# Down projections of a two-block transformer kernel: both classic output tiles in front of the Winograd groups in each first part

## The reference

```python
def sq_relu_mlp(x, w1, w2):
    h = jax.nn.relu(x @ w1)      # w1: 1024 x 4096
    return (h * h) @ w2          # w2: 4096 x 1024
```

```python
def swiglu(h, w_gate, w_up, w_down):          # width 2816
    return (jax.nn.silu(h @ w_gate) * (h @ w_up)) @ w_down
```

## Time and profile before

| | |
|---|---|
| median of 3 runs | 2046.54 us (2044.86 to 2048.42) |
| the profiled execution, its own time | 2046.04 us |
| its span in the trace | 2044.2 us |
| mean granted TensorE clock | 0.988 of full speed |
| PE, DVE, ACT busy | 96%, 70%, 46% of the span |
| DMA queues | 27.9% of 16 engines for the weights, mean 88 GB/s |

### The profile page before, as it was taken

How to read it: one execution, slowest core, us unless ns; L and a number is a source line. 1 busy time by engine, 2 the same in 40 slices (tenths; PEclk the granted TensorE clock), 3 DMA queues, 4 the chain that set the end, 5 groups by cost and what they waited for, 6 DMA issues and landing times. The chain is left out here.

```text
span 2044.2 us, 29741 instructions
## 1 busy us (share of the span) xinstructions
PE 1958.9 (96%) x11816; PEld 1070.4 (52%) x11821; DVE 1421.9 (70%) x2445; ACT 947.8 (46%) x1628; POOL 71.4 (3%) x51
## 2 busy tenths in 40 slices
PE   9989999999999999999999999999989999999997
PEld 4444444444444874444445844854544444476466
DVE  6979644548677677676587767769866646965777
ACT  4447733324333343346454434436467844643442
POOL 2000000000000102000000000000000000100000
PEclk9999999999999999999999999999989999999999
DMA  7300233324331343222221532316300031324321
GB/s 245 99 1 1 73 102 98 99 71 125 110 95 32 117 144 110 77 83 73 73 88 63 176 93 61 126 53 175 147 1 1 14 101 42 98 93 155 93 63 42
DMA packets 53931, 179.55 MB, mean 88 GB/s; under 512 B 6176, under 2 KB 11936, under 8 KB 53536
## 3 DMA queue, kind: packets, MB, share of 16 engines
q1 hardware_dynamic: 53792, 177.64, 27.9%
HBM read 174.47 MB, written 2.10 MB: 86 GB/s over the span
## 5 line engine op out<-in xcount | busy, mean ns | idle before, releaser
L2182 DVE SCALAR_TENSOR_TENSOR w_lo<-w_raw,w_hi 128x1024 f16<-128x1024 f32 (+3 forms) x359 | 452.1, 1266 | 82.9 <-ACT w_hi L1736 47.7
L1736 ACT ACTIVATE w_hi<-w_raw 128x1024 f16<-128x1024 f32 (+1 forms) x358 | 373.5, 1063 | 223.1 <-DVE w_raw L2202 84.6
L1171 PE MATMUL pS<-xx,w_hi 128*128 128x512 f16 x952 | 362.0, 380 | 5.1 <-DVE w_lo L2182 3.7
L1172 PE MATMUL pS<-xx,w_hi 128*128 128x512 f16 x952 | 362.0, 380 | 0.0
L1173 PE MATMUL pS<-xx,w_lo 128*128 128x512 f16 x952 | 361.9, 380 | 0.0
L1239 PE MATMUL pS<-arena,w_hi 128*128 128x256 f16 x645 | 178.0, 276 | 11.7 <-DVE arena L2775 5.1
L1241 PE MATMUL pS<-arena,w_lo 128*128 128x256 f16 x645 | 178.1, 276 | 0.0
L1240 PE MATMUL pS<-arena,w_hi 128*128 128x256 f16 x645 | 178.1, 276 | 0.0
L1171 PEld LDWEIGHTS pS<-xx,w_hi 128*128 128x128 f16 x952 | 93.4, 98 | 114.6 <-issue 5.6
L1173 PEld LDWEIGHTS pS<-xx,w_lo 128*128 128x128 f16 x952 | 93.3, 98 | 113.2 <-issue 1.5
L1172 PEld LDWEIGHTS pS<-xx,w_hi 128*128 128x128 f16 x952 | 93.3, 98 | 108.1 <-issue 1.9
(11 more groups left out here) (455 smaller groups left out, 3821.2 us busy)
## 6 DMA issues: line engine op xcount, KB each, us to landing
w_raw<-in_w SPq DMA_DIRECT2D x299, 512.0 KB, 3.8
w_raw<-in_w SPq DMA_DIRECT2D x12, 704.0 KB, 4.0
X<-in_x SPq DMA_DIRECT2D x8, 264.0 KB, 6.4
arena<-in_c SPq DMA_DIRECT2D x2, 1024.0 KB, 7.5
out_t<-X SPq DMA_DIRECT2D x16, 128.0 KB, 1.7
arena<-in_h SPq DMA_DIRECT2D x4, 256.0 KB, 12.5
arena<-in_h SPq DMA_DIRECT2D x2, 512.0 KB, 11.4
arena<-in_c SPq DMA_DIRECT2D x2, 256.0 KB, 2.9
```

The costliest lines, as they stand in the source:

```text
L1171: pe.matmul(ps, wh, ah, start=f, stop=False)
L1172: pe.matmul(ps, wh, al, start=False, stop=False)
L1736: act.activation(to_, from_, ACT.Copy, scale=WS).then_inc(hi_split, 1)
L2182: dve.scalar_tensor_tensor(out=lo_[:, a:], in0=from_[:, a:], scalar=WS, in1=hi_[:, a:], op0=ALU.mult, op1=ALU.subtract).then_inc(lo_split, 1)
```

## The change

- **a parts** (dn0a, dn1a): tile 7 becomes the second tile of the first classic stage. PE's order is now: tile 0, k 0 to 13; the second classic tile ("tile 1" of that stage), k 0 to 6; tile 0, k 14 and 15; the second tile, k 7 to 15; the three groups. Nothing stands behind the groups.
- **b parts and ffd**: tile 0 up to the last pair of k; product A11 of group 0, all but its last tile of k; tile 0's last pair; the rest of A11; the groups; tile 7 in halves as before.
- **Banks**: tile 0 of all five goes to bank 5 (pO), the second classic tile of the a parts to bank 3 (BANKS).
- **Weights**: the last unit of ffd7, up0a and up1a is closed at the stage's end (CLOSED), so the next stage starts a unit of its own. In the weight stream tile 7 of an a part stands behind tile 0.
- **Norms**: AHEAD["mb"] is 4 instead of 8, and in all of them the copy of the second half stands in front of the look-ahead splits instead of behind them (`formed`, the copy, `split_lo` instead of `out_of`, the copy).
- **Bias row**: `lay_bias` stands behind group 0 of dn0b on DVE, its high half there on ACT; ACT's wait for all operands ahead of a b part is gone.

The diff, cut where it only takes out what the functions above show:

```diff
@@ -74,3 +74,4 @@
 INSIDE = {"va": 0, "vb": NQ, "vm": 0, "vv": 0}
-BEHIND = ("dn0a7", "dn1a7")
+BANKS = {"ffd0": (5,), "dn0a0": (5, 3), "dn1a0": (5, 3), "dn0b0": (5,), "dn1b0": (5,)}
+CLOSED = ("ffd7", "up0a", "up1a")
 UP_A = 16
@@ -159,3 +160,4 @@
                     for kk in range(k):
-                        self.step(self.tau, kk == k - 1)
+                        ends = name in CLOSED and j == n - 1 and kk == k - 1
+                        self.step(self.tau, kk == k - 1, ends)
             else:
@@ -206,4 +208,4 @@
                     b = 4 + j if j < 2 else turn % 4
-                elif s.name in BEHIND:
-                    b = 4
+                elif s.name in BANKS:
+                    b = BANKS[s.name][j]
                 elif s.name in HOME:
@@ -275,4 +277,5 @@
 
-    def step(self, tau, last):
+    def step(self, tau, last, close=False):
         self.tile()
+        self.open = self.open and not close
         ends = not self.open
@@ -301,3 +304,5 @@
     k = UP_A if part == "a" else KFF2 - UP_A
-    return [(f"dn{lay}{part}0", "T", 1, k, 1), (f"dn{lay}{part}s", "S", 3, k // 2, 1), (f"dn{lay}{part}7", "T", 1, k, 1)]
+    if part == "a":
+        return [(f"dn{lay}a0", "T", 2, k, 1), (f"dn{lay}as", "S", 3, k // 2, 1)]
+    return [(f"dn{lay}b0", "T", 1, k, 1), (f"dn{lay}bs", "S", 3, k // 2, 1), (f"dn{lay}b7", "T", 1, k, 1)]
 
@@ -330,3 +335,3 @@
 DIRECT = ("x2", "ma", "mb", "mc", "md")
-AHEAD = {"x2": 8, "ma": 2, "mb": 8, "mc": 2, "md": 8}
+AHEAD = {"x2": 8, "ma": 2, "mb": 4, "mc": 2, "md": 8}
 HALVED = tuple(AHEAD)
@@ -1222,21 +1227,20 @@
 
-            def strassen(s, g, ops, copies, r):
...
+            def product(s, g, x, ops, copies, k0, k1):
+
+                name, b, op = PRODUCTS[x]
+                free = s.banks[g][b]
+                if name == "A12":
+                    pe.wait_ge(first_copied, copies + g + 1)
+                elif k0 == 0 and free >= 0:
+                    pe.wait_ge(evicted, free + 1)
+                ps = (pS[:, b, 0:HT] if b < 4 else (pT, pO)[b - 4][:, 0, 0:HT])
+                a = slice(op * HT, op * HT + HT)
+                for k in range(k0, k1):
+                    tau = s.factor(g, x, k)
+                    wh, wl = weights(tau)
+                    oh, ol = ops[0][:, k, a], ops[1][:, k, a]
+                    pe.matmul(ps, wh, oh, start=k == 0 and name != "A12", stop=False, skip_group_check=True)
+                    pe.matmul(ps, wh, ol, start=False, stop=False, skip_group_check=True)
+                    mm = pe.matmul(ps, wl, oh, start=False, stop=k == s.k - 1, skip_group_check=True)
+                if k1 == s.k:
                     mm.then_inc(mm_done, 1)
@@ -1249,9 +1253,19 @@
 
-                for k in range(parts[0].k):
-                    out_pair(parts[0], by_pairs(ops), k, r)
+                s, n = parts[0], parts[0].k
+                for k in range(n - 2):
+                    out_pair(s, by_pairs(ops), k, r)
+                if m is None:
+                    tile_T(s, 1, by_pairs(ops), 0, TPU - 1)
+                else:
+                    product(parts[1], 0, 0, ops, copies, 0, n // 2 - 1)
+                for k in range(n - 2, n):
+                    out_pair(s, by_pairs(ops), k, r)
+                if m is None:
+                    tile_T(s, 1, by_pairs(ops), TPU - 1, n)
                 for g in range(parts[1].n):
-                    strassen(parts[1], g, ops, copies, r + parts[0].k)
-                if m is None:
-                    out_T(parts[2], 0, by_pairs(ops))
-                else:
+                    for x in range(len(PRODUCTS)):
+                        if g == 0 and x == 1:
+                            pe.wait_ge(rhs_ready, r + n)
+                        product(parts[1], g, x, ops, copies, n // 2 - 1 if m is not None and g == 0 and x == 0 else 0, n // 2)
+                if m is not None:
                     out_last(parts[2], m, by_pairs(ops))
@@ -1260,14 +1274,5 @@
 
...
+                tile_T(s, 0, rhs, k, k + 1)
 
@@ -1652,3 +1657,3 @@
                     out_T(S[f"up{lay}a"], j, xr)
-                down([S[f"dn{lay}a{n}"] for n in "0s7"], hp, PL.r[h], 3 + 6 * lay)
+                down([S[f"dn{lay}a{n}"] for n in "0s"], hp, PL.r[h], 3 + 6 * lay)
                 for j in range(KFF2 - UP_A):
@@ -1748,3 +1753,4 @@
 
-                out_of(parts[0])
+                for j in range(parts[0].n):
+                    out_of(parts[0], j)
                 if m is not None:
@@ -1761,5 +1767,6 @@
                             square(PL.q[m] + n, out_to(m, n))
-                if m is None:
-                    out_of(parts[2])
-                else:
+                    if g == 0 and m == "mb":
+                        act.wait_ge(bias_laid, 1)
+                        hi(PL.r["pe"], z[0][:, 2, :], src[:, 1, :])
+                if m is not None:
                     halved_norm(parts[2], m)
@@ -2097,8 +2104,4 @@
                 up_part(S[f"up{lay}a"], lay, r, 0)
-                down([S[f"dn{lay}a{n}"] for n in "0s7"], 3 + 6 * lay, 1.0 / WS)
+                down([S[f"dn{lay}a{n}"] for n in "0s"], 3 + 6 * lay, 1.0 / WS)
                 up_part(S[f"up{lay}b"], lay, r, UP_A)
-                if lay == 0:
-                    act.wait_ge(bias_laid, 1)
-                    hi(PL.r["pe"], z[0][:, 2, :], src[:, 1, :])
-                act.wait_ge(rhs_ready, r + KFF2 + (lay == 0))
                 down([S[f"dn{lay}b{n}"] for n in "0s7"], 6 + 6 * lay, 1.0 / WS, m)
@@ -2807,4 +2810,5 @@
                 s = parts[0]
-                out_of(s)
-                taken_to(m, out_to(m, 0), out_bank(s.o0), f, to_add).then_inc(evicted, 1)
+                for j in range(s.n):
+                    out_of(s, j)
+                    taken_to(m, out_to(m, (0, KD - 1)[j]), out_bank(s.o0 + j), f, to_add).then_inc(evicted, 1)
                 s = parts[1]
@@ -2815,7 +2819,7 @@
                             add_square(m, n)
+                    if g == 0 and m == "mb" and squares:
+                        lay_bias()
+                if not squares:
+                    return
                 s = parts[2]
-                if not squares:
-                    out_of(s)
-                    taken_to(m, out_to(m, KD - 1), out_bank(s.o0), f, to_add).then_inc(evicted, 1)
-                    return
                 for n in (KD - 3, KD - 2):
@@ -2832,5 +2836,7 @@
                 if n == AMONG["x2"]:
-                    ps = out_of(s)
+                    formed(s, 0)
+                    ps = out_bank(s.o0)
                     dve.scalar_tensor_tensor(out=X[:, KD - 1, HT:T], in0=ps[:, HT:T], scalar=0.5 / WS, in1=X[:, KD - 1, HT:T],
                                              op0=ALU.mult, op1=ALU.add).then_inc(evicted, 1)
+                    split_lo(PL.out_tau[s.o0], most=splits(s, 0))
                 if n == KD - 1:
@@ -2937,3 +2943,3 @@
 
-                        out_of(s, s.n - 1)
+                        formed(s, s.n - 1)
                         if s.n == KD:
@@ -2941,2 +2947,3 @@
                         taken_to(m, m_view(m, KD - 1)[:, HT:T], out_bank(o)[:, HT:T], 1.0 / WS, s.n < KD).then_inc(evicted, 1)
+                        split_lo(PL.out_tau[o], most=splits(s, s.n - 1))
 
@@ -2998,6 +3005,4 @@
                 up_part(S[f"up{lay}a"], lay, h, 0)
-                down([S[f"dn{lay}a{n}"] for n in "0s7"], m, 3 + 6 * lay, 1.0 / WS, False)
+                down([S[f"dn{lay}a{n}"] for n in "0s"], m, 3 + 6 * lay, 1.0 / WS, False)
                 up_part(S[f"up{lay}b"], lay, h, UP_A)
-                if lay == 0:
-                    lay_bias()
                 down([S[f"dn{lay}b{n}"] for n in "0s7"], m, 6 + 6 * lay, 1.0 / WS, True, True)
@@ -3236,2 +3241,4 @@
         s[name + "0"], s[name + "7"], s[name + "s"] = w[:, :P], w[:, 7 * P:], w[:, P:7 * P]
+        if name[-1] == "a":
+            s[name + "0"] = np.concatenate([w[:, :P], w[:, 7 * P:]], 1)
     for st in PL.order:
```

More of the change, by code:

```diff
@@ L1221, in out_last @@
                     direct_norm(m)
-            def strassen(s, g, ops, copies, r):
-                free = s.banks[g]
-                for x, (name, b, op) in enumerate(PRODUCTS):
-                    if name == "A12":
-                        pe.wait_ge(first_copied, copies + g + 1)
-                    elif free[b] >= 0:
-                        pe.wait_ge(evicted, free[b] + 1)
-                    if g == 0 and x == 1:
-                        pe.wait_ge(rhs_ready, r)
-                    ps = (pS[:, b, 0:HT] if b < 4 else (pT, pO)[b - 4][:, 0, 0:HT])
-                    a = slice(op * HT, op * HT + HT)
-                    for k in range(s.k):
-                        tau = s.factor(g, x, k)
-                        wh, wl = weights(tau)
-                        oh, ol = ops[0][:, k, a], ops[1][:, k, a]
-                        pe.matmul(ps, wh, oh, start=k == 0 and name != "A12", stop=False, skip_group_check=True)
-                        pe.matmul(ps, wh, ol, start=False, stop=False, skip_group_check=True)
```

(26 more changed lines are left out.)

## The result

| | before | changed |
|---|---|---|
| median beside each other | 2046.54 us (5 runs, 2042.26 to 2048.42) | 2030.51 us (5 runs, 2026.54 to 2033.80) |
| ratio | | 0.9920, 95% interval 0.9905 to 0.9934 |
| profiled execution, span | 2046.04, 2044.2 us | 2030.51, 2028.7 us |
| mean granted clock | 0.988 | 0.991 |

What follows compares the result with a forecast made beforehand. PE, busy 96% of the span, was taken as the bound, leaving its idle and lower-clock time to win. 11.9 + 1.6 + 2.7 - 1.0 - 0.3 = 14.9, plus clock 2.3, is 17.2 us: 2046.0 to 2028.8, range 2025.0 to 2034.0.

Steps and rivals of the forecast that it cites:

- Pair and bank waits: First matmuls and last operand pairs of the four down parts: all six PE waits go, 11.9 us won.
- cv's tile 4: PE's wait there for a weight split goes once weight units are aligned with the stage: 1.6 us won.
- mb: Norm behind dn0b: copy ahead of two splits, four tiles ahead instead of eight, L2966 starts earlier: 2.7 us won.
- x2: Norm behind ffd: three splits now follow the copy of the second half, so L2846 starts later: 1.0 us lost.
- The bias row: Behind group 0 of dn0b, on ACT ahead of the copy for A12 of group 1: 0.3 us lost, bounds 0 and 2.2.
- The clock: Lower-clock falls behind dn0a, dn0b, dn1a gaps: 3.4 us of 5.1 won back, 1.1 lost at x2, net 2.3.
- Two thirds: Share of 1.7 us counted per clock fall; for x2's new 2.7 us gap ahead of cv, 1.1 us lost.
- three of three gaps above 2.2 us: Argument that gaps cause the clock falls: all three such gaps in the down parts were followed by one.
- against the first: Rival: the clock is not won back, only 14.9 us remain, 2031.1 us; chance 0.20.
- against the second: Rival: DVE bounds the a parts and the wait only moves; 6.5 us remain, 2039.5 us; chance 0.08.
- against the third: Rival: the second classic tile holds up the groups' weight splits; slower, 2050 us; chance 0.02.

Runs made afterwards that it cites:

- experiment 1: Kernel before with one edit, tile 0 of all five down parts to bank 5: 2032.94 us, one time.
- experiment 2: Changed kernel, a parts laid out like b parts: product A11 ahead of the last pair, second classic tile behind the groups in bank 4: 2030.84 us.
- experiment 4: Changed kernel, norm x2 alone in its old order: 5.54 us to cv's first matmul, 2030.25 in all; with two splits ahead of the copy 4.45.
- experiment 7: All of ffd's tile 0 before product A11, on the better version: 2023.05 us; on the changed kernel: 2027.74.
- Experiment 3: Changed kernel, norm mb's moves undone singly: 8 tiles ahead again, 8.65 us to kvc's first matmul; splits ahead of the copy again, 7.33.
- the better version: Changed kernel; x2 with two splits before the copy, 6 tiles ahead; mb 3 ahead; ACT's bias half behind A12's copy: 2024.93 us.
- experiment 6: Repeated timing of the better version, 2024.93 us (6 runs), beside the unedited change, 2028.55, and the kernel before, 2046.08.
- the second of experiment 3: Changed kernel, norm mb with splits ahead of the copy again and 4 tiles ahead: 7.33 us from PE's last matmul to kvc's first.

## Why the prediction was right

- **Pair and bank waits, 11.9 us, right.** All are gone; 2.09 + 2.70 + 2.48 + 0.91 + 2.69 + 0.95 = 11.82. The cover was far larger than needed: bank 3 was free 4.0 us ahead where I had 1.5. DVE took the last up tile 4.6 us behind the up part's last matmul instead of 7.1, about a split and a sum of weights (1.2 us each) sooner. The change's headline is not what paid: experiment 1 puts 8.8 of the 11.8, and the clock behind them, on the bank, and experiment 2 finds the second classic tile no better than product A11.
- **cv's tile 4, 1.6, right**: 1.58, and the wait there is gone. No run closes the units alone, but the stretch was 59.42 in both profiles with the old units and 57.84 in all twelve with the new ones, also with x2's old order (experiment 4) and ffd's (experiment 7).
- **mb, 2.7, right**: L2973 started 3.99 us behind PE's last matmul where 4.01 was worked out. Experiment 3 shows that it takes both moves.
- **x2, 1.0 lost, right**: 0.99. The 2.00 us of DVE's idle time ahead of the copy was there to be read from the order and would have given the better version at once.
- **The bias row, 0.3, right in its place, a little low here**: 0.53 at A12 of group 1, as named; 0.29 to 0.53 in nine profiles.
- **The clock, 2.3 net: the mechanism right, the sum off and partly luck.** The three falls behind the gaps went (5.1, I counted 3.4). Against that stood x2's (1.7, I counted 1.1) and ffd's (1.7, not counted). That makes 1.7. The mixer of layer 1, untouched, was 1.7 shorter by chance, which makes 3.4 in all. "Two thirds" for x2 was too much by what the runs show: one profile of six. And "three of three gaps above 2.2 us" was too short a list: behind ffd the trace before has seven such gaps, all with a fall. One is 2.51 us in the norm mb (0.50 for 3.4 us from 1345.5), which the change removes; it cost nothing, because PE ran only fillers there and then waited.
- **Not foreseen**: 1.36 us of waiting in ffd for a load, and 1.05 at the start. Both differ between profiles whose code is the same there: the wait was 1.00 to 2.82, and the first matmul of the projections came at 7.99 to 9.33. They are not what the change is worth.
- **The sum.** 11.82 + 1.58 + 2.69 - 0.99 - 0.53 + 3.4 is 18.0; less 1.36 and 1.05 it is 15.6, where the two profiled executions differ by 15.5 and the forecast had 17.2. Without the mixer's 1.7 these two executions would differ by 13.8. The medians are the sounder comparison: they lie 16.0 us apart in the result and 17.5 in experiment 6, and the forecast's 17.2 lies between.
- **The rivals.** The clock was won back, against the first: no fall is left in the down parts, in any of the twelve profiles of the change and its variants, and none was there in experiment 1, where only the bank waits had gone. (The page "TensorE: Matmul & The Clock Gate" of the Trainium skill, "Why this matters for your kernels", warns of longer gaps only; the runs disagree, with falls behind gaps of 2.48 and 2.70 us that are gone when the gaps are.) The waits did not move, against the second. The splits of the groups were not held up, against the third: no wait for them stands in the down parts, and DVE even idled 4.22 us ahead of tile 0's copy.

## What to carry to other kernels

A wait for a bank that is wanted next is the cheapest to remove: look at which buffer the next consumer takes before reordering work. When a late engine's chain sets a stage's start, list what it does between the last input and the first output, and move what isn't needed to where it would idle, ahead or behind; one rule for all such places costs at those where the idle time lies on the other side. Fillers that are to keep the clock up stand on the path themselves once it has fallen: nine of them took 3.7 us instead of 2.1 in experiment 3 and held up the next stage by 0.6.

## What the runs showed of the hardware

A gap of the same length at the same place is followed by the lower clock in some executions and not in others: 2.8 us in front of cv in one profile of six, 2.3 to 2.8 us in ffd in five of nine. Other places are steadier: 2.51 us in the norm mb in three profiles of three (before, experiment 1, the second of experiment 3), 3.8 us in the mixer of layer 1 in thirteen of fourteen. A gap of 2.10 us that ended at 904.04 in the kernel before never was (14 profiles), nor 2.0 in front of kvc (7 profiles), nor 2.09 alone in dn0a in experiment 1. In the kernel before that same gap in dn0a had one of 2.70 behind it, with 1.1 us of work between, and then the clock fell, and in the mixer of layer 1 it fell behind some of 1.8 to 2.0 us as well. Length alone does not decide. Behind a gap in steady work one fall cost 1.7 us, so the clock's price is best counted as a share of 1.7 us per gap, with the scatter of the runs to match.

The same load of 704 KB, issued at the same point of the program, landed 5.3 to 5.6 us later in five profiles and 6.6 to 7.1 us later in nine.
